# The end of the front stage of a hybrid attention and DeltaNet layer in another order: value tiles, late strips, packed rows and stores

## The chip, the cores and the metric

The kernel runs on one core of a Trainium2 chip. The time is that of one execution on the device, in microseconds (us). A core has a matrix engine (TensorE, PE in the profile, with its weight loads as PEld), a vector engine (VectorE, DVE), a scalar engine (ScalarE, ACT), GpSimd (POOL) and a queue engine that issues transfers (SyncE, SP). The engines run side by side, each works through its own list of instructions in order, and they wait for each other by semaphores.

## What is computed

One layer of a flow-matching backbone, in fp32, over 256 context tokens and 1024 latent tokens (1280 in all, model width 1024). The conditioning vectors give six modulation vectors per token group (`mod = silu(cond) @ w_mod + b_mod`), and one combined projection feeds two mixers:

```
h    = rmsnorm(x, norm_mix) * (1.0 + scale1) + shift1
proj = h @ w_in            # aq, ak, av, dq, dk, dv, dbeta, dalpha, dgate, g_attn, g_dn
aq, ak = rmsnorm per head;  latent tokens also get the axial rotation
o_attn = softmax(rot(aq) @ [cached keys, rot(ak)].T / 8) @ [cached values, av]
o_dn   = gated DeltaNet, both directions, chunks of 64
x = x + gate1 * (sigmoid(g_attn) * (o_attn @ w_attn_br) + sigmoid(g_dn) * (o_dn @ w_dn_br)) @ w_out
x = x + gate2 * moe(rmsnorm(x, norm_ffn) * (1.0 + scale2) + shift2)   # 16 experts, 2 per token
```

The outputs are the final norm of x, and the context tokens' keys, values and DeltaNet states.

## The kernel before

The program is cut into stages. At the end of a stage every engine adds 1 to the semaphore `arrivals` and waits until all five have done so: this is a barrier. Only the **front stage** and its barrier (the first one, `arrivals` 5) are touched. The **attention stage** follows behind it.

The front stage normalises and turns x into `hT` (tokens along the free axis), and makes the first third of the modulation. Then come five tiles of 128 columns of `w_in` (NA = 5: one of keys, `ak`, four of queries, `aq`). A tile goes through these steps:

- `gemm(n)` on PE, line 800; ACT copies the product to SBUF (L1272) and squares it (L1282).
- `ssq(n)` on PE, L826: the sums of squares by head, three column groups of 256, 512 and 512. `roots(n)` on ACT, L1248: their square roots. It waits until tile n-1 is done.
- `norm_tile(n)` on DVE: a reciprocal (L1540), the scaled tile (L1545, signal `y_ready`). `rotate(n)` on PE (L832, two groups of 512) needs that signal. Then DVE multiplies each half with the sine (L1552, signal `rot_used`), multiplies the tile with the cosine (L1554) and adds (L1556, signal `tile_done`).

Beside this run ten **value tiles**, `values_betas(n)` on PE (L847, 16 instructions each: 8 matmuls, in two passes each), which ACT copies out (L1298, L1299). They depend on `hT` and on free PSUM banks alone.

The rest of the modulation comes in eight **late strips**, numbers 4 to 11 of 12. Each is a transfer of 2 MB into one buffer, `wmod_late`, issued by SP (L472) when PE has used the strip before it (`wmod_used`). `late_mod(j)` on PE first turns the result of strip j-1 (`mod_turn`, L732, after ACT has copied it, L1208) and then multiplies strip j (`mod_rows`, L725). `late_mod(12)` turns the last. With that DVE finishes the modulation and packs the rows that later stages need into `row_pack` (L1492, L1496, L1566). PE turns the pack (L879, signal `rows_turned`), DVE copies it (L1576, `mod_ready` 4), and SP stores it in `row_scratch` (L527).

PE also turns the 512 cached keys (L872, needs the last value tile copied) and the context part of the new keys (L876, needs `tile_done` of the last tile). DVE copies both (L1569, and L1572 to `ktok`, which SP stores as an output, L525).

The order of all this is written out by hand. On PE, before: all five tiles with strips 4 to 8 between them; value tiles 0 and 1; `rotate(3)` and `ssq(4)`; value tile 2; then strips 9, 10, 11 behind value tiles 2, 5 and 8; value tile 9; `late_mod(12)`; `rotate(4)`; the turns. SP at the end waits for its stores to land (`sp_out` 64 and `rows_in` 16) before it arrives at the barrier.

Of the kernel before, what the change touches and what calls it, by code (L numbers as in the profile page):

```python
# [19 lines left out]
ACT = mybir.ActivationFunctionType  # L20
AX = mybir.AxisListType

P = 128
# [71 lines left out]
def build(nc, a, outs):  # L95
    ctx = ExitStack()
    with ctx:
# [133 lines left out]
        NA = 5  # L231

        def strips_in(n):
            return 16 * sum(2 if TILES[m][0] == "aq" else 1 for m in range(n % NW, n + 1, NW))
# [45 lines left out]
        ktok = R3[:, 1024:1024 + 2 * P].rearrange("p (n c) -> p n c", c=P)  # L280
# [189 lines left out]
        def _(sp):  # L470
# [50 lines left out]
            for g in range(2):  # L521
                sp.dma_start(outs[3][0, 0, g].rearrange("(n p) d -> p n d", p=P), v_sb[:, 0:2, g * HD:(g + 1) * HD]).then_inc(S["sp_out"], 16)
            sp.wait_ge(S["dve_once"], 3)
            for g in range(2):
                sp.dma_start(outs[2][0, 0, g].rearrange("(n p) d -> p n d", p=P), ktok[:, :, g * HD:(g + 1) * HD]).then_inc(S["sp_out"], 16)  # L525
            sp.wait_ge(S["mod_ready"], 4)
            sp.dma_start(rows_d, pack_turned).then_inc(S["rows_in"], 16)  # L527
            sp.wait_ge(S["sp_out"], 64)
            sp.wait_ge(S["rows_in"], 16)
# [11 lines left out]
            sp.wait_ge(S["sp_out"], 192)  # L541

# [167 lines left out]
        def _(pe):  # L710
# [50 lines left out]
            def late_mod(j):  # L761
                if j - 1 >= EARLY:
                    mod_turn(j - 1, 7, P)
                if j < NMOD:
                    mod_rows(j, 7)
# [94 lines left out]
            for n in range(NT):  # L860
                values_betas(n)
                if n == 1:
                    rotate(NA - 2)
                    ssq(NA - 1)
                if n % 3 == 2:
                    late_mod(EARLY + NA + n // 3)
# [6 lines left out]
            last.then_inc(S["pe_once"], 1)  # L873
            pe.wait_ge(S["tile_done"], NA)
# [3 lines left out]
            pe.wait_ge(S["mod_ready"], 3)  # L878
            mm(ps[0:64, 0, 0:P], row_pack, ident, start=True, stop=True).then_inc(S["rows_turned"], 1)  # L879
# [318 lines left out]
        def _(act):  # L1198
# [3 lines left out]
            def mod_rows(j, bank):  # L1202
                act.wait_ge(S["wmod_used"], j + 1)
                if j - 1 > 0:
                    act.wait_ge(S["mod_turned"], j)
                for q in range(4):
                    r = slice(32 * q, 32 * q + 2)
                    f(mod_row[r, j % 2, :], ps[r, bank, 0:P], ACT.Copy).then_inc(S["mod_row"], 1)  # L1208
# [96 lines left out]
            for n in range(NT):  # L1305
                values_betas(n)
                if n == 3:
                    roots(NA - 1)
                if n % 3 == 2:
                    mod_rows(EARLY + NA + n // 3, 7)  # L1310
# [168 lines left out]
        def _(dve):  # L1479
# [55 lines left out]

            def norm_tile(n):
# [10 lines left out]

                dve.wait_ge(S["past_in"], 96)
# [12 lines left out]
            dve.wait_ge(S["mod_turned"], NMOD + 1)  # L1561
            modulation(4 * EARLY, 4 * NMOD, ps[:, 7, P + 8 * EARLY:P + 8 * NMOD])
            scale_of(A2, 32, norm_ffn)
            for r, src in enumerate((mod[:, 16:24, :], A2[:], mod[:, 24:32, :], mod[:, 40:48, :])):
                signal = "mod_ready" if r == 3 else "dve_chain"
                v.tensor_copy(row_pack[:, 16 * r:16 * r + 16].rearrange("p (c k) -> p k c", c=2), src).then_inc(S[signal], 1)  # L1566
                dve.wait_ge(S[signal], 3 if r == 3 else count(signal))
            dve.wait_ge(S["pe_once"], 1)
            v.tensor_copy(kT[:, T:T + PAST], ps[:, 2, :]).then_inc(S["dve_chain"], 1)  # L1569
            dve.wait_ge(S["dve_chain"], count("dve_chain"))  # L1570
            dve.wait_ge(S["pe_once"], 2)
            v.tensor_copy(flat(ktok), ps[:, 3, 0:2 * P]).then_inc(S["dve_once"], 1)  # L1572
            dve.wait_ge(S["dve_once"], count("dve_once"))

            dve.wait_ge(S["rows_turned"], 1)
            v.tensor_copy(pack_turned, ps[0:64, 0, 0:P]).then_inc(S["mod_ready"], 1)  # L1576
            dve.wait_ge(S["mod_ready"], 4)
# [656 lines left out]
```

## Times and profile before

| | us |
|---|---|
| median of 3 runs | 2327.17 |
| lowest, highest | 2324.61, 2339.4 |
| profiled execution | 2330.84 |
| its span | 2328.9 |
| PE busy in the span | 2119.4 (91%) |
| DVE busy | 992.8 (43%) |
| ACT busy | 627.9 (27%) |
| POOL busy | 251.0 (11%) |

The span is the time from the first to the last instruction of the profiled execution; the rest of its own time lies around it. All times inside are counted from the span's start. PE's granted clock, as a share of full speed, was 0.958 in the mean. Where a row of the trace lists idle time in brackets, that is the engine's idle time just before the row's first instruction, and what ended it.

### The profile page before, as it was taken

How to read it: one execution, taken by the hardware profiler on the slowest of the kernel's cores; microseconds unless marked ns; L12 is line 12 of the kernel's file. 1: busy time of each engine (PE TensorE's matmuls, PEld its weight loads, DVE VectorE, ACT ScalarE, POOL GpSimd, SP SyncE). 2: the span in 40 equal slices, each digit the busy share in tenths (PEclk: the TensorE clock that was granted, in tenths of full speed). 3: DMA queues.
4: the chain of work that ended last, by engine and by line, in shares of the span. 5: the costliest groups of instructions: out<-in, count | busy, mean ns of one | idle time of the engine just before them, and what ended most of it. 6: DMA issues, size and time to landing. Idle time of an engine off the chain costs nothing. (4 is left out here: it accounts for less than half of the span.)

```text
span 2328.9 us, 39352 instructions
## 1 busy us (share of the span) xinstructions
PE 2119.4 (91%) x16471; PEld 1295.2 (56%) x16471; DVE 992.8 (43%) x1846; ACT 627.9 (27%) x1292; POOL 251.0 (11%) x311
## 2 busy tenths in 40 slices
PE   4996899999998889998899999999999689989993
PEld 3555567766554478887654555555455544434441
DVE  3254565652776476667460111001233423323334
ACT  6222666663343233332330000000111011111113
POOL 2000000000000133342000000000000012212220
PEclk8998899999999999999999999999999589999997
DMA  9422200001100223433302211111422656787846
GB/s 332 150 94 90 58 4 2 2 1 55 27 23 5 39 48 65 74 61 51 84 0 73 51 31 27 27 27 46 155 83 98 226 151 171 194 242 207 241 85 207
DMA packets 256381, 210.09 MB, mean 90 GB/s; under 512 B 147468, under 2 KB 219472, under 8 KB 255568
## 3 DMA queue, kind: packets, MB, share of 16 engines
q1 hardware_dynamic: 244912, 168.66, 24.6%
q0 software_dynamic: 11296, 38.92, 7.4%
q8 instruction: 133, 2.18, 0.4%
q14 instruction: 40, 0.33, 0.0%
HBM read 160.14 MB, written 47.25 MB: 89 GB/s over the span
## 5 line engine op out<-in xcount | busy, mean ns | idle before, releaser
L800 PE MATMUL ps<-R 128*128 128x512 f32 (+1 forms) x816 | 297.4, 522 | 5.0 <-DVE R L1526 1.9
L1076 PE MATMUL ps<-R 128*128 128x512 f32 (+1 forms) x768 | 279.5, 522 | 4.4 <-POOLq L2186 2.3
L1160 PE MATMUL ps<-R 128*128 x560 | 255.4, 610 | 16.2 <-SPq L691 13.9
L800 PEld LDWEIGHTS ps<-R 128*128 128x128 f32 x816 | 154.3, 190 | 144.5 <-issue 133.7
L1076 PEld LDWEIGHTS ps<-R 128*128 128x128 f32 x768 | 145.3, 190 | 136.1 <-issue 126.3
L1160 PEld LDWEIGHTS ps<-R 128*128 128x128 f32 x560 | 109.1, 196 | 156.8 <-issue 156.8
L1850 DVE TENSOR_TENSOR R<-ps,R 128x512 f32<-128x512 f32 (+1 forms) x48 | 28.9, 603 | 376.8 <-ACT R L1426 376.0
L1589 DVE TENSOR_SCALAR_CACHE_REDUCE R<-ps 128x512 f32<-128x512 f32 (+1 forms) x208 | 128.4, 666 | 60.1 <-PE ps L896 60.0
L968 PE MATMUL ps<-R 64*64 64x64 f32 x3840 | 130.0, 225 | 24.7 <-DMA R<-tu_scratch 13.0
L968 PEld LDWEIGHTS ps<-R 64*64 64x64 f32 x3840 | 122.8, 140 | 42.5 <-issue 13.7
L1101 PE MATMUL ps<-R 128*128 128x512 f32 x320 | 141.2, 600 | 3.9 <-PEq L1088 3.9
L1081 PE MATMUL ps<-R 128*128 128x512 f32 (+1 forms) x384 | 141.7, 521 | 0.5 <-DMA R<-attn_out_scratch 0.5
L2196 POOL DMA_INDIRECT R<-h_scratch,slot_i x35 | 34.4, 982 | 928.7 <-DVE slot_i L2010 729.3
L1426 ACT ACTIVATE R<-ps 128x512 f32<-128x512 f32 (+1 forms) x48 | 25.2, 526 | 395.1 <-PE ps L1081 394.3
L1170 PE MATMUL ps<-R 128*128 x280 | 126.2, 593 | 1.6 <-DVE R L2053 1.6
L915 PEld LDWEIGHTS ps<-cst,R 128*128 128x128 f32 x800 | 86.4, 142 | 58.9 <-issue 49.7
L2053 DVE COPY R<-ps 128x256 f32<-128x256 f32 x35 | 14.9, 424 | 236.0 <-PE ps L1185 236.0
L915 PE MATMUL ps<-cst,R 128*128 128x128 f32 x800 | 105.1, 279 | 5.7 <-ACT R L1330 2.9
L896 PE MATMUL ps<-R 64*128 64x512 f32 (+1 forms) x416 | 106.5, 616 | 3.5 <-SPq L531 3.3
L1320 ACT ACTIVATE R<-R 128x1536 f32<-128x1536 f32 (+1 forms) x80 | 108.6, 1358 | 3.0 <-DVE R L1598 2.9
L1081 PEld LDWEIGHTS ps<-R 128*128 128x128 f32 x384 | 72.9, 190 | 65.4 <-issue 61.2
L1464 ACT ACTIVATE R<-ps 128x256 f32<-128x256 f32 x35 | 13.4, 384 | 342.7 <-PE ps L1160 342.7
(288 smaller groups left out, 2800.0 us busy)
## 6 DMA issues: line engine op xcount, KB each, us to landing
R<-in_w_mod_dram SPq DMA_DIRECT2D x12, 2048.0 KB, 9.1
R<-in_w_gate_e_dram SPq DMA_DIRECT2D x16, 1024.0 KB, 5.8
R<-in_w_up_e_dram SPq DMA_DIRECT2D x16, 1024.0 KB, 11.2
R<-in_w_down_e_dram SPq DMA_DIRECT2D x16, 1024.0 KB, 13.2
R<-in_w_in_dram SPq DMA_DIRECT2D x30, 512.0 KB, 5.4
R<-tu_scratch SPq DMA_DIRECT2D x80, 128.0 KB, 3.3
R<-in_x_sample_dram SPq DMA_DIRECT2D x16, 512.0 KB, 6.3
lt_scratch<-R SPq DMA_DIRECT2D x40, 128.0 KB, 2.8
```

What stands on the lines that cost most here:

```text
L800: last = mm(ps[:, u % 4, 0:w], w_sb[n % NW][:, k, :], hT[:, k, c0:c0 + w], start=(k == 0), stop=(k == KD - 1))
L896: last = mm(ps[:, 2 * (u % 2) + g, 0:w], qT[lo, h4, qt * P:(qt + 1) * P], kT[lo, c0 + j * 512:c0 + j * 512 + w], start=True, stop=True)
L915: last = turn128(ps[:, 4 + v % 3, k * P:(k + 1) * P], s_sb[i % 2][g][:, j * 512 + k * P:j * 512 + (k + 1) * P], ident)
L968: last = mm(ps[lo, bank, a * C:(a + 1) * C], lhs(a)[lo], rhs(a)[lo], start=start and (alone or a == 0), stop=stop and (alone or a == PAIRS ...
L1076: mm(ps[:, o + x, 0:w], wk[:, x, k, :], hT[:, k, c0:c0 + w], start=(k == 0), stop=(k == KD - 1))
L1081: last = mm(ps[:, o + 2 + x, 0:w], wb[:, x, k, :], (aoT, odT)[x][:, k, c0:c0 + w], start=(k == 0), stop=(k == 3))
L1101: last = mm(ps[:, 2 * (n % 2) + h, :], mT[:, k, n * P:(n + 1) * P], ow[k][:, h * 512:(h + 1) * 512], start=(k == 0), stop=(k == KD - 1))
L1160: last = mm(ps[:, 2 + t % 2, :], hsT[t % 2][:, k, :], R[:, bass.ds(at + (RB + k * 512), 512)], start=(k == 0), stop=(k == KD - 1))
L1170: last = mm(ps[:, 5 + u % 3, :], hidT[t % 2][:, k, :], R[:, bass.ds(at + (RB + 4096 + k * D + h * 512), 512)], start=(k == 0), stop=(k == 1))
L1320: f(s_sb[i % 2][g][:, 0:w], s_sb[i % 2][g][:, 0:w], ACT.Exp, bias=shift[i % 2][g], accum_out=sums[qt % 2][:, g, h4:h4 + 1]).then_inc(S["p_ ...
L1589: v.tensor_scalar(s_sb[i % 2][g][:, j * 512:j * 512 + w], ps[:, 2 * (u % 2) + g, 0:w], HD ** -0.5, None, ALU.mult, ALU.max, accum_out=tops ...
L2196: pool.indirect_dma_start(hs[t % 2], None, h2_d, bass.IndirectOffsetOnAxis(ap=slot_i[:, t:t + 1], axis=0)).then_inc(S[f"hs_in{t % 2}"], 16)
```

## The change

Five things are moved, and one instruction pair is added.

1. PE and ACT: a table `LATE_BEHIND` puts strips 9, 10 and 11 behind value tiles 3, 6 and 9 (before: 2, 5 and 8), and `rotate(3)` with `ssq(4)`, and on ACT `roots(4)`, go behind value tile 4 (before: PE behind value tile 1, ACT behind 3).
2. DVE: finishing the modulation and packing its rows is now a function `rows_modulated()`, called in the last tile's `norm_tile` before its rotation, no longer behind it.
3. PE turns the pack before it turns the context keys; DVE copies the pack before `ktok`; SP stores the pack first.
4. SP no longer waits for its stores before the first barrier. It waits for the rows one barrier later. The buffer of `ktok` moves to a place that the attention stage doesn't write.
5. ACT: an `Exp` of one column, and the wait for it, before the barrier.

```diff
+        LATE_BEHIND = {3: EARLY + NA, 6: EARLY + NA + 1, 9: EARLY + NA + 2}
...
-        ktok = R3[:, 1024:1024 + 2 * P].rearrange("p (n c) -> p n c", c=P)
+        ktok = R3[:, 15040:15040 + 2 * P].rearrange("p (n c) -> p n c", c=P)
@@ sync: the pack's store goes ahead of ktok's
+            sp.wait_ge(S["mod_ready"], 4)
+            sp.dma_start(rows_d, pack_turned).then_inc(S["rows_in"], 16)
             sp.wait_ge(S["dve_once"], 3)
             for g in range(2):
                 sp.dma_start(outs[2][0, 0, g]...ktok...).then_inc(S["sp_out"], 16)
-            sp.wait_ge(S["mod_ready"], 4)
-            sp.dma_start(rows_d, pack_turned).then_inc(S["rows_in"], 16)
-            sp.wait_ge(S["sp_out"], 64)
-            sp.wait_ge(S["rows_in"], 16)
             sp.sem_inc(S["arrivals"], 1)
...
             sp.wait_ge(S["sp_out"], 192)
+            sp.wait_ge(S["rows_in"], 16)
@@ tensor
             for n in range(NT):
                 values_betas(n)
-                if n == 1:
+                if n in LATE_BEHIND:
+                    late_mod(LATE_BEHIND[n])
+                if n == 4:
                     rotate(NA - 2)
                     ssq(NA - 1)
-                if n % 3 == 2:
-                    late_mod(EARLY + NA + n // 3)
             late_mod(NMOD)
             rotate(NA - 1)
...
+            pe.wait_ge(S["mod_ready"], 3)
+            mm(ps[0:64, 0, 0:P], row_pack, ident, start=True, stop=True).then_inc(S["rows_turned"], 1)
             pe.wait_ge(S["tile_done"], NA)
             for n in range(2):
                 last = turn128(ps[:, 3, n * P:(n + 1) * P], kT[:, n * P:(n + 1) * P], ident)
             last.then_inc(S["pe_once"], 1)
-            pe.wait_ge(S["mod_ready"], 3)
-            mm(ps[0:64, 0, 0:P], row_pack, ident, start=True, stop=True).then_inc(S["rows_turned"], 1)
@@ scalar
             for n in range(NT):
                 values_betas(n)
-                if n == 3:
+                if n in LATE_BEHIND:
+                    mod_rows(LATE_BEHIND[n], 7)
+                if n == 4:
                     roots(NA - 1)
-                if n % 3 == 2:
-                    mod_rows(EARLY + NA + n // 3, 7)
+            f(stat[:, 63:64], one_c, ACT.Exp).then_inc(S["act_chain"], 1)
+            act.wait_ge(S["act_chain"], count("act_chain"))
@@ vector: the body of rows_modulated() stood behind the loop over norm_tile
+                if n == NA - 1:
+                    rows_modulated()
                 dve.wait_ge(S["past_in"], 96)
                 for g in (1, 2):
                     dve.wait_ge(S["rot_mm"], 2 * n + g)
```

On PE, from the first value tile to the turn of the last strip. `R` is the large SBUF buffer, `ps` PSUM; L847 is a value tile (x16 is two tiles of 8 matmuls), L732 a turn, L725 a strip, L832 a rotation, L826 the sums of squares. Before:

```order
L847 MATMUL ps<-R 128x160 x16
L832 MATMUL ps<-R,cst 128x512 x2
L826 MATMUL ps<-R,cst 128x256
L826 MATMUL ps<-R,cst 128x512 x2
L847 MATMUL ps<-R 128x160 x8
L732 MATMUL ps<-cst,mod_row 128x8
L725 MATMUL ps<-R,cond_s 2x128 x32
L847 MATMUL ps<-R 128x160 x24
L732 MATMUL ps<-cst,mod_row 128x8
L725 MATMUL ps<-R,cond_s 2x128 x32
L847 MATMUL ps<-R 128x160 x24
```

And after the change, where every line number of this part is one higher:

```order
L848 MATMUL ps<-R 128x160 x32
L733 MATMUL ps<-cst,mod_row 128x8
L726 MATMUL ps<-R,cond_s 2x128 x32
L848 MATMUL ps<-R 128x160 x8
L833 MATMUL ps<-R,cst 128x512 x2
L827 MATMUL ps<-R,cst 128x256
L827 MATMUL ps<-R,cst 128x512 x2
L848 MATMUL ps<-R 128x160 x16
L733 MATMUL ps<-cst,mod_row 128x8
L726 MATMUL ps<-R,cond_s 2x128 x32
L848 MATMUL ps<-R 128x160 x24
```

Value tiles 2, 3 and 4 and strip 9 now stand ahead of the rotation of tile 3. Behind the last rows shown come, before, the last strip, a value tile, the last turn and the last rotation; after, the last strip, the last turn and the last rotation, with no value tile between.

On DVE, the last tile from its reciprocal on, and the packing (L1492 to L1566 before). Before:

```order
L1540 RECIPROCAL R<-R 128x1280 [waits root_ready,tile_done]
L1545 SCALAR_TENSOR_TENSOR R<-R,prm 128x256 [waits dve_chain]
L1545 SCALAR_TENSOR_TENSOR R<-R,prm 128x1024 [waits dve_chain]
L1552 TENSOR_TENSOR R<-ps,R 128x512 [waits rot_mm,past_in,y_ready]
L1552 TENSOR_TENSOR R<-ps,R 128x512 [waits rot_mm,rot_used]
L1554 TENSOR_TENSOR R<-R 128x1024 [waits rot_used]
L1556 TENSOR_TENSOR R<-R 128x1024 [waits dve_chain]
L1492 TENSOR_TENSOR mod<-ps,prm 128x64 [waits mod_turned,tile_done]
```

After:

```order
L1552 RECIPROCAL R<-R 128x1280 [waits root_ready,tile_done]
L1557 SCALAR_TENSOR_TENSOR R<-R,prm 128x256 [waits dve_chain]
L1557 SCALAR_TENSOR_TENSOR R<-R,prm 128x1024 [waits dve_chain]
L1495 TENSOR_TENSOR mod<-ps,prm 128x64 [waits mod_turned,y_ready]
L1499 SCALAR_TENSOR_TENSOR A<-mod,prm 128x16 [waits dve_chain]
L1545 COPY R<-mod 128x8x2 [waits dve_chain]
L1545 COPY R<-A 128x8x2 [waits dve_chain]
L1545 COPY R<-mod 128x8x2 [waits dve_chain] x2
L1566 TENSOR_TENSOR R<-ps,R 128x512 [waits rot_mm,past_in,mod_ready]
```

The six small instructions of the packing, and their wait for the last strip's turn (`mod_turned`), now stand between the scaled tile and its rotation's products.

On SP, from the stores of the context values to the first load of the attention stage. Before:

```order
L522 DMA out_dram<-R 128x2x64
L525 DMA out_dram<-R 128x2x64 [waits dve_once]
L525 DMA out_dram<-R 128x2x64
L527 DMA row_scratch<-R 64x128 [waits mod_ready]
L501 DMA R<-in_w_in_dram 128x8x128 [waits sp_out,rows_in,arrivals]
```

After:

```order
L524 DMA out_dram<-R 128x2x64
L526 DMA row_scratch<-R 64x128 [waits mod_ready]
L529 DMA out_dram<-R 128x2x64 [waits dve_once]
L529 DMA out_dram<-R 128x2x64
L503 DMA R<-in_w_in_dram 128x8x128 [waits arrivals]
```

The store of the pack is first, and the first load behind the barrier no longer waits for stores.

## Rows read from the trace of the kernel before

**Rows 1.** Busy time by stretch: start:end, length, engines' busy us, granted clock, DMA share, GB/s.

```profile
172.59:237.97 65.38, 43.67 (x389) 35.01 (x389) 32.37 (x25) 14.45 (x48) 0.00 (x0) 0.83 0.28 96
237.97:560.00 322.03, 314.39 (x2886) 216.06 (x2887) 186.78 (x591) 198.97 (x351) 21.49 (x27) 0.99 0.07 20
```

**Rows 2.** Timeline of PE: start us, us, operation, count, idle before it and its end.

```profile
174.81 4.51 PE L847 MATMUL ps<-R 128*128 128x160 f32 x32
188.45 3.74 PE L832 MATMUL ps<-R,cst 128*128 128x512 f32 x4 [9.13 <-DVE R L1545]
193.13 2.39 PE L826 MATMUL ps<-R,cst 128*128 128x256 f32 x6 [0.94 <-DVE R L1552]
...
197.53 0.28 PE L732 MATMUL ps<-cst,mod_row 128*128 128x8 f32 x2
197.74 1.93 PE L725 MATMUL ps<-R,cond_s 128*2 128x128 f32 x64
...
208.78 3.37 PE L725 MATMUL ps<-R,cond_s 128*2 128x128 f32 x64 [2.27 <-DMA R<-in_w_mod_dram]
...
221.41 2.39 PE L725 MATMUL ps<-R,cond_s 128*2 128x128 f32 x64 [2.24 <-DMA R<-in_w_mod_dram]
...
227.31 1.96 PE L832 MATMUL ps<-R,cst 128*128 128x512 f32 x4
...
237.97 2.08 PE L896 MATMUL ps<-R 64*128 64x256 f32 x8 [3.30 <-SPq L531]
```

**Rows 3.** Timeline of DVE in the same stretch.

```profile
192.29 0.69 DVE L1552 TENSOR_TENSOR R<-ps,R 128x512 f32<-128x512 f32 x1 [0.94 <-PE ps L832]
...
194.28 1.22 DVE L1556 TENSOR_TENSOR R<-R 128x1024 f32<-128x1024 f32 x1
204.35 8.15 DVE L1540 RECIPROCAL R<-R 128x1280 f32<-128x1280 f32 x1 [8.84 <-ACT R L1248]
212.54 1.81 DVE L1545 SCALAR_TENSOR_TENSOR R<-R,prm 128x256 f32<-128x256 f32 x2
228.55 1.52 DVE L1552 TENSOR_TENSOR R<-ps,R 128x512 f32<-128x512 f32 x2 [14.21 <-PE ps L832]
...
232.62 0.22 DVE L1492 TENSOR_TENSOR mod<-ps,prm 128x64 f32<-128x64 f32 x1
...
233.96 0.69 DVE L1569 COPY R<-ps 128x512 f32<-128x512 f32 x1
234.68 0.42 DVE L1572 COPY R<-ps 128x256 f32<-128x256 f32 x1
235.14 0.28 DVE L1576 COPY R<-ps 64x128 f32<-64x128 f32 x1
```

**Rows 4.** Timeline of ACT in the same stretch.

```profile
202.33 1.92 ACT L1248 ACTIVATE R<-ps,epsc 128x256 f32<-128x256 f32 x3
...
223.84 1.14 ACT L1208 ACTIVATE mod_row<-ps 2x128 f32<-2x128 f32 x4 [4.39 <-PE ps L725]
```

**Rows 5.** Timeline of SP's queue in the same stretch.

```profile
199.73 12.82 SPq L472 DMA_DIRECT2D R<-in_w_mod_dram  x2
...
235.13 0.89 SPq L525 DMA_DIRECT2D out_dram<-R  x2
236.06 0.54 SPq L527 DMA_DIRECT2D row_scratch<-R  x1
```

**Rows 6.** DMA issues of 150 to 262 us: KB each, median us from issue to landing.

```profile
row_scratch<-R SPq DMA_DIRECT2D x1, 32.0 KB, 1.8
```

**Rows 7.** Timeline of ACT, first rows behind the barrier.

```profile
240.26 1.28 ACT L1320 ACT_TABLE_LOAD   x1 [12.53 <-DVE R L1598]
241.56 0.51 ACT L1320 ACTIVATE R<-R 128x256 f32<-128x256 f32 x1
```

**Rows 8.** Timeline of PE behind the barrier.

```profile
242.21 1.18 PE L915 MATMUL ps<-cst,R 128*128 128x128 f32 x4 [2.17 <-ACT R L1320]
243.32 1.22 PE L896 MATMUL ps<-R 64*128 64x256 f32 x4
...
246.57 0.71 PE L896 MATMUL ps<-R 64*128 64x256 f32 x4
...
248.46 0.70 PE L896 MATMUL ps<-R 64*128 64x256 f32 x4
```

**Rows 9.** Busy time by stretch, columns as in group 1: clock before and behind the barrier.

```profile
234.00:236.00 2.00, 0.67 (x2) 0.27 (x2) 1.35 (x3) 0.00 (x0) 0.00 (x0) 0.50 0.00 0
...
248.00:250.00 2.00, 1.98 (x18) 1.07 (x20) 0.76 (x8) 1.89 (x8) 0.11 (x1) 1.00 1.19 291
```

More of the change, by code:

```diff
@@ L1534, in _, with rows_modulated @@
             SEG = [(0, 256, 1), (256, 1024, 259)]
+            def rows_modulated():
+                dve.wait_ge(S["mod_turned"], NMOD + 1)
+                modulation(4 * EARLY, 4 * NMOD, ps[:, 7, P + 8 * EARLY:P + 8 * NMOD])
+                scale_of(A2, 32, norm_ffn)
+                for r, src in enumerate((mod[:, 16:24, :], A2[:], mod[:, 24:32, :], mod[:, 40:48, :])):
+                    signal = "mod_ready" if r == 3 else "dve_chain"
+                    v.tensor_copy(row_pack[:, 16 * r:16 * r + 16].rearrange("p (c k) -> p k c", c=2), src).then_inc(S[signal], 1)
+                    dve.wait_ge(S[signal], 3 if r == 3 else count(signal))
             def norm_tile(n):
@@ L1560, in _ @@
                 norm_tile(n)
[L1561 to L1567, printed above, removed]
             dve.wait_ge(S["pe_once"], 1)
@@ L1570, in _ @@
             dve.wait_ge(S["dve_chain"], count("dve_chain"))
+            dve.wait_ge(S["rows_turned"], 1)
+            v.tensor_copy(pack_turned, ps[0:64, 0, 0:P]).then_inc(S["mod_ready"], 1)
+            dve.wait_ge(S["mod_ready"], 4)
             dve.wait_ge(S["pe_once"], 2)
@@ L1573, in _ @@
             dve.wait_ge(S["dve_once"], count("dve_once"))
-            dve.wait_ge(S["rows_turned"], 1)
-            v.tensor_copy(pack_turned, ps[0:64, 0, 0:P]).then_inc(S["mod_ready"], 1)
-            dve.wait_ge(S["mod_ready"], 4)
             dve.sem_inc(S["arrivals"], 1)
```

## The prediction

> **What bounds the kernel now.** I read the page first: PE is busy 91% of the span. The table of stretches shows where it is not: in the last 65.38 us of the front stage, from the sums of squares of tile 3 to the first scores of attention, PE is busy 43.67 us, and 21.7 us are idle; in the 322.03 us behind it, it is busy 314.39 [rows 1]. So what this stage loses is lost to the kernel, and what is saved here is kept as long as the next stages are bound by PE and by nothing that runs on a clock of its own. I then read the timelines of PE, DVE, ACT and SP side by side.
>
> PE's idle pieces are: 9.13 us for the scaled tile 3, 0.94 for its rotation's products, 2.27 and 2.24 for strips, and at the end the wait for DVE and the stores, of which 3.30 us stand in front of the first scores and name SP [rows 2]. Two chains lead to the barrier. The **tile chain**: tile 3 done at 195.50 (194.28 + 1.22), roots of tile 4 only at 202.33, reciprocal at 204.35, scaled tile at 214.35 (212.54 + 1.81), and then DVE idles 14.21 us because PE comes to `rotate(4)` only at 227.31 [rows 2 to 4]. The **strip chain**: strip 10 is issued at 199.73 and used from 208.78, 9.05 us later; strip 11 is issued at about 212.2 (the end of that row's 12.82 us, less an issue) and used from 221.41, 9.2 us later [rows 2, 5]. PE's own order holds both: `rotate(4)` stands behind all value tiles and strips, and strip 9 is used at 197.74 though PE idled before 188.45. The attention stage then begins with a table load on ACT, 1.28 us, and PE waits 2.17 us for that exponential [rows 7, 8].
>
> **The change step by step.** Times are worked out on this trace's axis.
>
> *The 9.13 us gap is filled.* A value tile takes 4.51 / 2 = 2.26 us, turn and strip together 2.1 us (from 197.53 to 199.67) [rows 2]. From 174.81: four value tiles to 183.85, strip 9 to 185.95, value tile 4 to 188.2. The scaled tile 3 comes when it did, and PE rotates at 188.45. So 8.9 us of work move into idle time and delay nothing, with 0.25 us to spare. If the cover were too short, the excess would be paid once in the tile chain only.
>
> *Rotation of tile 3 at full clock.* Behind the gap it took 3.74 us; `rotate(4)` out of a busy stretch took 1.96 [rows 2]. By the second, the first product is there 1.24 us after the start (227.31 to 228.55), and DVE needs 4.07 us from there until it is free again (228.55 to 232.62) [rows 2, 3]. Tile 3 is done at 188.45 + 1.24 + 4.05 = 193.7, 1.8 us sooner.
>
> *Tile 4.* `ssq(4)` follows at 191.35 and ends at 193.75 (2.39 us); the roots need tile 3 done, and now stand behind value tile 4's copy, long past. They take 1.92 us to 195.7 [rows 2, 4]. Reciprocal and scaling take 10.0 us (204.35 to 214.35) [rows 3]: scaled tile at 205.8, 8.5 us sooner.
>
> *The strips.* Strip 10 is issued when strip 9 is used, 185.95, and lands by 195. PE goes on at 193.75: value tiles 5 and 6 to 198.2, strip 10 to 200.3. Strip 11 is issued there and lands 9.05 to 9.2 us later, 209.4. Value tiles 7 to 9 take PE to 207.1, so it waits 2.2 us, as it does now. The strip took 3.37 and 2.39 us behind such waits [rows 2]; I take 2.9: 212.3. ACT's copy takes 1.14 [rows 4] and nothing covers it any more, since value tile 9 has gone ahead: 213.5. The turn is there at 213.7, against 227.4 now. That is the pacemaker of the new order: the strip chain, not the tile chain, which has been ready for 8 us.
>
> *Packing ahead of the last rotation.* It costs DVE 1.34 us (232.62 to 233.96) [rows 3] whichever way; now it lies beside `rotate(4)`, whose first product needs 1.24 us. DVE begins on the products at 215.05 and is free at 219.1, if the array runs at full clock. At half clock the second product comes 3.84 us after the start (188.45 to 192.29) [rows 2, 3], and this step is 1.6 us longer. PE is busy from 209.4 but for 1.2 us, so I take the first.
>
> *The tail.* DVE still has the copies of the cached keys, the pack and `ktok`: 0.69, 0.28 and 0.42 us [rows 3], with gaps 1.5 us, to 220.6. What PE turns in between is covered by them: the pack during the tile's last two products, the keys during the first copy. SP issues the pack's store (0.54) at 220.1 and `ktok`'s two (0.89) from 220.7 [rows 5], and arrives at 221.6. It waits for no landing, where now the barrier opens only when the store issued at 236.06 has landed, 1.8 us later [rows 5, 6]. First scores at 221.8 instead of 237.97: **16.2 us**. Queued behind these stores are only loads that the DeltaNet stage uses, and the new wait for the rows stands behind a wait for eight transfers that SP issues in the middle of attention: both nothing. The moved `ktok` costs nothing.
>
> *The table load.* ACT has nothing to do from 215 to 221.8, so a load and an `Exp` of one column are covered there. PE's wait of 2.17 us behind the barrier shrinks by the load, **1.3 us** [rows 7, 8]; were the cover gone it would be worth nothing, not less. Behind it ACT uses exponential and copies as before.
>
> The Trainium skill ("ScalarE: Activation LUTs", section "What ACT_TABLE_LOAD costs") gives 1283 ns for the load and about 1380 ns for a drain, 2.66 us for a switch. The trace agrees on the load and shows no drain on this path: the load starts at 240.26, and the exponential at 241.56. By the page the sum would be 1.4 us larger; I take the row.
>
> *The clock at the start of attention.* It is at half (1.2 GHz) from before the barrier on and back at full (2.4 GHz) by 248 [rows 9]. At half, one round from scores to scores took 3.25 us (243.32 to 246.57), at full 1.9 (246.57 to 248.46) [rows 8]. PE goes into the barrier as idle as now, so I take no change; a round sooner or two is 1.3 to 2.6 us of gain, a round later 1.3 of loss.
>
> Sum: 16.2 + 1.3 = 17.5 us. Against the profiled execution's own time, 2330.84, that is 2313.3. That execution lies 3.7 us above the median of 2327.17, and the change is compared with such medians: 2327.17 - 17.5 = 2309.7, said as **2310**. Its own range: the upper side has the half clock (1.6), the strip at 3.37 us (0.5), a later clock (1.3) and the median's own place (lowest run 2324.61, highest 2339.4); the lower side the earlier clock (2.6) and the lowest run (2.6). That gives 2305 to 2315.
>
> **The rivals.**
>
> *The late strips pace it worse than worked out.* Everything behind strip 11 now hangs on a 9 us transfer with no work beside it but three value tiles, and DVE holds the finished tile 4 back until its turn. For it: both strips are waited for already [rows 2]. Against it: the load has its queue alone, and took 9.05 and 9.2 us. With a strip of 11 us twice, the half clock and the longer strip, the gain falls to 17.5 - 2 - 1.6 - 0.5 - 1, about 12.5: 2315. Chance 0.13.
>
> *Nothing is kept.* The barrier opens earlier, but the attention or a later stage runs into a date that doesn't move. For it there is no row: all five engines start the attention stage from the barrier, SP loads for it nothing, and PE is at 314.39 of 322.03 [rows 1]. The same result would come if another engine reached the barrier late. 2326. Chance 0.05.
>
> *More is kept.* The filled gap and the shorter wait keep the array's clock high into the attention stage, two rounds of 1.3 us at its start, and a drain that the trace hides goes as well: 17.5 + 4 = 21.5, 2305.5. Chance 0.10.
>
> *Slower.* The place is the start of the attention stage: the clock does not come back there. A round costs 1.3 us more at half clock [rows 8], so it takes 14 such rounds in a row to eat the 17.5 us, and more from there on to be slower; with 20 rounds the time is 2310 + 26 = 2336. For it: one of three runs of the same kernel took 2339.4, so some executions lose 12 us somewhere. Against it: the mean granted clock of the stretch behind the barrier is 0.99, the cold start included [rows 1], and its work isn't changed. Chance 0.03.
>
> **How the numbers follow.** The forecast has 0.69, the rivals 0.13, 0.05, 0.10 and 0.03. The likeliest time is 2310. The range starts at 2304, just below the case where more is kept, and ends at 2317, above the case of slow strips; it leaves out the case where nothing is kept, the slower one, and the tails. A measurement of this kernel can tell about 1%, 23 us, from no change. The whole sum is 0.75% of the time, so within 1% has nearly everything: faster by over 1% would need 2303.9 or less, a tail of the case where more is kept, 0.04; slower by over 1% needs 2350, 0.02; within 1%, 0.94.
>
> **What would show it.** In the changed profile PE should have no idle of more than 1 us between 174.8 and 188.4, and the rotation of tile 3 should take about 2 us instead of 3.74. The reciprocal of tile 4 should start near 195.8, strip 11 should be used from near 209.4 with 2 us of wait before it, the last rotation start near 213.6, and the first scores near 221.8, released by SP or DVE; the table load should stand before the barrier, and PE's wait behind the first scores be 0.9 us. The prediction is wrong if value tiles 2 to 4 overrun 188.45 by more than 1 us, if a strip's load takes well over 9.2 us now that it starts at another time, if the first scores move by 16 us and the last instruction does not, or if the clock behind the barrier differs by more than two rounds.

## The result and the profile after

The median after the change is 2315.36 us (6 runs, 2311.09 to 2316.06), beside 2330.94 us before (6 runs, 2324.61 to 2339.4). The medians are 15.6 us apart. The ratio found by comparing the runs is 0.9925, with a 95% interval of 0.9908 to 0.9942: a gain of 17.5 us, 13.5 to 21.4. The profiled execution took 2312.47 us, 18.4 us less than that of before. The forecast was 2310 us, with a sum of 17.5 us.

First the busy time by stretch: from the sums of squares of tile 3 to the first scores, and the same length behind them as in [rows 1]. The columns are start:end, length, busy us of PE, PEld, DVE, ACT and POOL, granted clock, DMA share, GB/s.

```profile
172.37:220.27 47.90, 38.34 (x389) 32.12 (x389) 32.36 (x25) 15.95 (x50) 0.00 (x0) 0.98 0.37 128
220.27:542.30 322.03, 315.59 (x2888) 216.64 (x2889) 186.76 (x591) 197.68 (x350) 21.49 (x27) 0.99 0.07 20
```

The stretch is 17.48 us shorter (65.38 to 47.90) with the same 389 matmul instructions. PE's idle time in it fell from 21.7 to 9.6 us, 12.1 us less. The other 5.3 us are busy time, 43.67 to 38.34: the same work at a granted clock of 0.98 instead of 0.83. The stretch behind it has the same granted clock in both, 0.99; PE is busy 1.2 us more in the same length. I call the start of the sums of squares of tile 3 **the mark** (172.59 before, 172.37 here), since executions differ by up to 3 us ahead of it (171.93 to 174.85 in all profiles of this text).

PE's timeline after the change, from the mark:

```profile
172.37 2.39 PE L827 MATMUL ps<-R,cst 128*128 128x256 f32 x6 [0.94 <-DVE R L1566]
174.59 8.86 PE L848 MATMUL ps<-R 128*128 128x160 f32 x64
...
183.50 1.93 PE L726 MATMUL ps<-R,cond_s 128*2 128x128 f32 x64
185.35 2.44 PE L848 MATMUL ps<-R 128*128 128x160 f32 x16
188.22 1.98 PE L833 MATMUL ps<-R,cst 128*128 128x512 f32 x4 [0.43 <-DVE R L1557]
...
208.46 1.93 PE L726 MATMUL ps<-R,cond_s 128*2 128x128 f32 x64 [1.76 <-DMA R<-in_w_mod_dram]
211.65 0.39 PE L733 MATMUL ps<-cst,mod_row 128*128 128x8 f32 x2 [1.26 <-ACT mod_row L1209]
211.90 1.96 PE L833 MATMUL ps<-R,cst 128*128 128x512 f32 x4
...
217.47 0.44 PE L879 MATMUL ps<-cst,R 128*128 128x128 f32 x2 [2.81 <-DVE R L1570]
220.27 2.08 PE L897 MATMUL ps<-R 64*128 64x256 f32 x8 [2.35 <-SPq L531]
223.23 1.18 PE L916 MATMUL ps<-cst,R 128*128 128x128 f32 x4 [0.89 <-ACT R L1323]
224.34 1.22 PE L897 MATMUL ps<-R 64*128 64x256 f32 x4
```

Against [rows 2]: the gap of 9.13 us is 0.43; the rotation behind it takes 1.98 us, no longer 3.74; only one strip is waited for, 1.76 us, and the wait for ACT's copy that follows, 1.26 us, is new. Behind the first scores PE waits 0.89 us for ACT, where it waited 2.17 [rows 8]; the next scores (L897) still take 1.22 us, the half clock.

DVE, around the last tile and the packing:

```profile
195.57 8.15 DVE L1552 RECIPROCAL R<-R 128x1280 f32<-128x1280 f32 x1 [2.05 <-ACT R L1249]
...
212.15 0.23 DVE L1495 TENSOR_TENSOR mod<-ps,prm 128x64 f32<-128x64 f32 x1 [6.58 <-PE ps L733]
...
213.48 1.42 DVE L1566 TENSOR_TENSOR R<-ps,R 128x512 f32<-128x512 f32 x2
...
218.49 0.42 DVE L1582 COPY R<-ps 128x256 f32<-128x256 f32 x1
```

The reciprocal starts 8.8 us sooner than in [rows 3]. DVE then has the scaled tile at 205.57 and waits 6.58 us for the last strip's turn.

SP and ACT at the end of the stage:

```profile
218.49 0.54 SPq L526 DMA_DIRECT2D row_scratch<-R  x1
219.07 1.09 SPq L529 DMA_DIRECT2D out_dram<-R  x2
220.28 7.49 SPq L503 DMA_DIRECT2D R<-in_w_in_dram  x6
```

```profile
210.46 1.14 ACT L1209 ACTIVATE mod_row<-ps 2x128 f32<-2x128 f32 x4 [3.47 <-PE ps L726]
211.62 1.28 ACT L1312 ACT_TABLE_LOAD   x1
212.91 0.20 ACT L1312 ACTIVATE stat<-epsc 128x1 f32<-128x1 f32 x1
```

SP's last issue ends at 220.16, and the first load behind the barrier starts at 220.28: nothing waits for a landing. The table load has moved from the first softmax [rows 7] into ACT's idle time.

### The profile page after: what moved, and what is told of

Its sections match the earlier page's. It is cut to its first block and busy times, and to the rows that moved or that the text cites. A ratio compares the mean times of both kernels' runs of the same rounds, so it can differ in the third digit from the quotient of the medians.

```text
span 2310.5 us, 39353 instructions
## 1 busy us (share of the span) xinstructions
PE 2116.4 (92%) x16471; PEld 1296.2 (56%) x16471; DVE 993.0 (43%) x1846; ACT 628.1 (27%) x1293; POOL 250.1 (11%) x311
## 3 DMA queue, kind: packets, MB, share of 16 engines
q8 instruction: 133, 2.18, 0.4%
## 5 line engine op out<-in xcount | busy, mean ns | idle before, releaser
L897 PE MATMUL ps<-R 64*128 64x512 f32 (+1 forms) x416 | 106.9, 618 | 2.5 <-SPq L531 2.4
```

The lines of the kernel that those rows point to most:

```text
L897: last = mm(ps[:, 2 * (u % 2) + g, 0:w], qT[lo, h4, qt * P:(qt + 1) * P], kT[lo, c0 + j * 512:c0 + j * 512 + w], start=True, stop=True)
```

## The experiments

Places are given from each run's own mark, so that the different starts drop out. The table has the three places that matter; all come from PE's timelines.

| kernel | last rotation | first scores | from rotation to scores | PE's wait for ACT behind them |
|---|---|---|---|---|
| before | 54.72 | 65.38 | 10.66 | 2.17 |
| before, second profile | 55.53 | 66.19 | 10.66 | 2.17 |
| changed | 39.53 | 47.90 | 8.37 | 0.89 |
| changed, second and third profile | 39.75, 39.22 | 48.12, 47.59 | 8.37, 8.37 | 0.89, 0.89 |
| order on PE and ACT alone | 39.66 | 50.32 | 10.66 | 2.16 |
| stores alone | 52.56 | 62.03 | 9.47 | 2.17 |
| changed, no table load ahead | 39.42 | 47.80 | 8.38 | 2.17 |
| changed, packing behind | 39.86 | 49.41 | 9.55 | 0.89 |
| changed, strip 10 early | 36.38 | 44.75 | 8.37 | 0.89 |
| the same, last rotation early, packing behind | 33.96 | 43.44 | 9.48 | 0.89 |
| before, last rotation moved alone | 46.15 | 58.76 | 12.61 | 2.17 |

### The order alone

```diff
 the kernel before, with
+        LATE_BEHIND = {3: EARLY + NA, 6: EARLY + NA + 1, 9: EARLY + NA + 2}
 and the changed loops over values_betas on PE and on ACT; nothing else
```

> The kernel before with the new order on PE and ACT alone (strips 9, 10, 11 behind value tiles 3, 6, 9; rotation and sums behind value tile 4); packing, stores and table load as before. Measured from the start of the sums of squares of tile 3, the first scores came 65.4 us later before and 47.9 us later after the change. Theory (the order on PE is nearly the whole gain): the last rotation starts as in the changed kernel, 39.5 us behind that mark; from the first product on DVE to the first scores it takes 9.4 us as before, so the first scores come at 39.5 + 1.2 + 9.4 = 50.2 us, a gain of 15.3 of the 17.5. Rival (the stores' landings and the packing are a large part): first scores at 54 or later. PE's wait for ACT behind the first scores stays 2.2 us.

PE's timeline of this run:

```profile
213.12 1.96 PE L834 MATMUL ps<-R,cst 128*128 128x512 f32 x4
...
223.78 2.08 PE L898 MATMUL ps<-R 64*128 64x256 f32 x8 [3.30 <-SPq L533]
```

The first scores stand 50.32 us behind the mark, 0.1 from the theory. From the rotation to them it takes the same 10.66 us as before, and the 3.30 us of [rows 2] are there to the hundredth. The order on PE and ACT is worth 15.06 of the 17.48 us. Which part of that is PE's order and which is ACT's (`roots(4)` on ACT started only at 202.33 [rows 4], although tile 3 was done at 195.50 [rows 3]) no run separates. The execution took 2317.47 us.

### The stores alone

```diff
 the kernel before, with
+        ktok = R3[:, 15040:15040 + 2 * P]...
 the pack turned, copied and stored ahead of ktok, and
-            sp.wait_ge(S["sp_out"], 64)
-            sp.wait_ge(S["rows_in"], 16)
```

> The kernel before with the stores' part alone: the pack turned, copied and stored first, no wait for landings before the barrier, ktok's buffer moved; order on PE and ACT, packing behind the last tile and table load as before. Theory: the barrier's opening moves by the landing less what the stores' issue still costs: DVE done at 235.4, the last store issued by 236.5, first scores at 236.6 instead of 237.97, so 64.0 us behind the mark instead of 65.4, a gain of 1.4. Rival (the stall is worth the whole 3.3 us that PE spends for SP): first scores 62.1 us behind the mark.

```profile
208.24 0.28 PE L731 MATMUL ps<-cst,mod_row 128*128 128x8 f32 x2
210.55 3.37 PE L724 MATMUL ps<-R,cond_s 128*2 128x128 f32 x64 [2.02 <-DMA R<-in_w_mod_dram]
...
227.41 1.96 PE L831 MATMUL ps<-R,cst 128*128 128x512 f32 x4
...
236.88 2.08 PE L895 MATMUL ps<-R 64*128 64x256 f32 x8 [1.97 <-SPq L529]
```

Read from the mark, 62.03 is the rival's number, 62.1. It is the wrong ruler here, and the expectation should not have used it: the edit touches nothing ahead of the last rotation, yet that stands at 52.56 instead of 54.72 in this execution (shorter waits for strips, 2.02 and 2.20 us, and, at full clock this time, the last strip with 1.93 us instead of 2.39 and above all the value tile behind it with 2.44 instead of 3.61). Behind the rotation, where the edit lies, 10.66 us became 9.47: the stores' part is worth 1.19 us. PE's wait marked with SP fell from 3.30 to 1.97 and did not vanish, since PE waits there for DVE's copies and SP's issues too. The Trainium skill ("DMA: Bandwidth & Descriptors", section "Rules for kernel authors") says to wait on a transfer's semaphore late, so that its fixed cost overlaps. The runs agree on the direction; of the 1.8 us from issue to landing [rows 6] 1.19 came back. The rest is mostly the issue itself, 0.54 us, which still has to be done: SP's last issue ends 1.25 us behind DVE's last copy here (235.53 to 236.78), 1.18 before (235.42 to 236.60).

### The changed kernel without the table load ahead

```diff
 the changed kernel, without
-            f(stat[:, 63:64], one_c, ACT.Exp).then_inc(S["act_chain"], 1)
-            act.wait_ge(S["act_chain"], count("act_chain"))
```

> The changed kernel without the Exp of one column. Theory: first scores stay 47.9 us behind the mark, the table load of 1.28 us is again behind them, and PE's wait for ACT there is 2.2 us instead of 0.9; everything behind is 1.3 us later. Rival (a drain of another 1.4 us is paid at such a switch, or the load is covered by DVE's reductions): the wait grows by 2.7 us, or not at all.

ACT's timeline, and then PE's:

```profile
222.67 1.28 ACT L1321 ACT_TABLE_LOAD   x1 [10.97 <-DVE R L1602]
223.97 0.51 ACT L1321 ACTIVATE R<-R 128x256 f32<-128x256 f32 x1
```

```profile
220.38 2.08 PE L897 MATMUL ps<-R 64*128 64x256 f32 x8 [2.36 <-SPq L531]
224.62 1.18 PE L916 MATMUL ps<-cst,R 128*128 128x128 f32 x4 [2.17 <-ACT R L1321]
```

The load is worth 1.28 us in PE's wait, 2.17 against 0.89. The expectation's "everything behind is 1.3 us later" was too much: from the first scores to the last of the stage it takes 295.4 us here and 294.6 in the changed kernel, 0.8 more. The rival with a drain, which the Trainium skill ("ScalarE: Activation LUTs", section "What ACT_TABLE_LOAD costs") puts at about 1380 ns on top, is refuted for this place: the exponential starts 0.02 us behind the load, and the load starts as soon as DVE's row maximum for the softmax is there. This execution took 2309.89 us, less than the changed kernel's 2312.47, although it lost 1.28 us here. A single execution can't show such a term; its place in the trace can.

### The packing behind the last tile again

```diff
 the changed kernel, with rows_modulated() called behind the loop over norm_tile:
-                if n == NA - 1:
-                    rows_modulated()
```

> The changed kernel with the packing behind the last tile's rotation again (order of PE and ACT, stores and Exp as changed). Theory: the packing's 1.34 us lie beside the rotation's first product in the changed kernel and on the path here; the products start 0.3 us sooner, so the first scores come 1.0 us later, 48.9 us behind the mark. Rival (DVE is not on the path to the barrier, SP is): no change, 47.9.

```profile
212.73 1.96 PE L833 MATMUL ps<-R,cst 128*128 128x512 f32 x4
...
222.28 2.08 PE L897 MATMUL ps<-R 64*128 64x256 f32 x8 [1.57 <-SPq L531]
```

From the rotation to the first scores it takes 9.55 us instead of 8.37: the packing ahead of the rotation's products is worth 1.18 us. DVE is on the path to the barrier. The place from the mark, 49.41, is 0.5 later than expected; 0.33 of that is the last rotation's own place in this execution.

### Strip 10 early

```diff
 the changed kernel, with
-        LATE_BEHIND = {3: EARLY + NA, 6: EARLY + NA + 1, 9: EARLY + NA + 2}
+        LATE_BEHIND = {3: EARLY + NA, 8: EARLY + NA + 2}
                 if n == 4:
                     rotate(NA - 2)
                     ssq(NA - 1)
+                    late_mod(EARLY + NA + 1)
 and the same on ACT
```

> The changed kernel with another order on PE and ACT: strip 10 right behind the sums of squares of tile 4 (in the changed kernel behind value tile 6), strip 11 behind value tile 8 (there behind 9). Theory (the chain of late strips paces the new order): strip 11 is issued 4.4 us sooner and lands before PE has done value tiles 5 to 8, so PE's wait of 1.8 us for it is gone, and value tile 9 covers ACT's copy of its result, so most of the 1.3 us wait for ACT is gone too: last rotation 2.7 us sooner, first scores about 45.2 us behind the start of the sums of squares of tile 3 instead of 47.9. Rival (the chain of tile 4 through ACT and DVE paces): the last rotation stays where it is, 39.5 us behind the mark, or moves by less than 0.5 us. In time 2.7 us is 0.12%, at the edge of what five rounds can tell.

```profile
193.98 1.93 PE L726 MATMUL ps<-R,cond_s 128*2 128x128 f32 x64
195.84 8.96 PE L848 MATMUL ps<-R 128*128 128x160 f32 x64
204.64 0.28 PE L733 MATMUL ps<-cst,mod_row 128*128 128x8 f32 x2
204.85 1.93 PE L726 MATMUL ps<-R,cond_s 128*2 128x128 f32 x64
206.71 2.44 PE L848 MATMUL ps<-R 128*128 128x160 f32 x16
208.99 0.28 PE L733 MATMUL ps<-cst,mod_row 128*128 128x8 f32 x2
209.13 1.96 PE L833 MATMUL ps<-R,cst 128*128 128x512 f32 x4
```

No row in this stretch has idle time ahead of it: both waits, 1.76 and 1.26 us, are gone, and the last rotation and the first scores stand 3.15 us sooner. In the changed kernel the chain of late strips was the pacemaker, not tile 4. The median is 2310.31 us (2306.87 to 2315.63, 5 runs), the ratio to before 0.9910 (0.9897 to 0.9924).

### The last rotation early as well

```diff
 the kernel above, with
                 if n in LATE_BEHIND:
                     late_mod(LATE_BEHIND[n])
+                if n == NT - 2:
+                    rotate(NA - 1)
...
             late_mod(NMOD)
-            rotate(NA - 1)
 and the packing behind the last tile again
```

> The kernel of the early strip with the last rotation behind strip 11 and ahead of value tile 9 and the last turn, and the packing behind the tile's rotation. Theory (the scaled tile 4 lies ready for 3 us and more before PE comes to it): rotation 2.3 us sooner again, the packing's 1.3 us back on DVE's path behind it: first scores 1.0 us sooner than with the early strip alone, 44.2 us behind the mark, 3.7 us sooner than in the changed kernel. Rival (the last strip's turn decides whatever stands where): no gain over the early strip alone, or a loss of up to 1.3 us.

```profile
208.48 1.98 PE L833 MATMUL ps<-R,cst 128*128 128x512 f32 x4
210.30 2.34 PE L848 MATMUL ps<-R 128*128 128x160 f32 x16
...
217.96 2.08 PE L899 MATMUL ps<-R 64*128 64x256 f32 x8 [1.99 <-SPq L531]
```

The mark of this run is 174.52. The first scores stand at 43.44, another 1.31 us sooner. In DVE's timeline the scaled tile 4 is ready 33.22 us behind the mark, and the rotation starts at 33.96: the last rotation now follows tile 4 by 0.74 us, so the next thing in the way is the tile chain itself.

That lead is not kept through the attention stage. The same instructions there, behind the same wait, in the kernel with the early strip alone and then in this one:

```profile
280.94 1.50 PE L917 MATMUL ps<-cst,R 128*128 128x128 f32 x12 [1.83 <-ACT R L1335]
281.92 2.62 PE L918 MATMUL ps<-cst,R 128*128 128x128 f32 x12 [1.83 <-ACT R L1336]
```

The granted clock is 1.00 behind the first wait (281 to 285) and 0.53 and then 0.62 behind the second (282 to 284, 284 to 286). The second profile of this kernel has the same dip (2.79 us for these instructions, clock 0.55 and 0.60); the other eleven profiles take 1.50 us there. The last scores of the stage start 340.3 us behind the mark here, 339.5 with the early strip alone and 342.5 in the changed kernel. So at the end of the scores the early rotation is 0.8 us behind the early strip alone, and its lead over the changed kernel is 2.2 us. Why the clock falls there only with this order was not tried.

The median is 2306.58 us (2301.92 to 2309.3, 4 runs), the ratio 0.9881 (0.9866 to 0.9897).

### The last rotation moved alone

```diff
 the kernel before, with
+                if n == 8:
+                    rotate(NA - 1)
...
             late_mod(NMOD)
-            rotate(NA - 1)
```

> The kernel before with one call moved: the last rotation on PE stands behind value tile 8 instead of behind the last strip's turn. Nothing is filled into the gap ahead of tile 3's rotation, strips and stores as before. Theory (the two chains meet at PE's own order): DVE finishes tile 4 while PE waits for strip 11, so the last turn, 54.6 us behind the start of the sums of squares of tile 3, is followed at once by the packing, and from the packing's start to the first scores it takes 5.35 us as before: first scores 60.0 us behind the mark instead of 65.4. The remaining 12 us to the changed kernel are then the strips' own lateness, which only the filled gap takes away. Rival (order around the last tile is worth most of the gain): first scores 55 us behind the mark or sooner; or nothing at all, 65.4.

```profile
218.86 1.88 PE L832 MATMUL ps<-R,cst 128*128 128x512 f32 x4
...
221.59 1.93 PE L725 MATMUL ps<-R,cond_s 128*2 128x128 f32 x64 [0.73 <-DMA R<-in_w_mod_dram]
...
231.47 2.08 PE L897 MATMUL ps<-R 64*128 64x256 f32 x8 [3.55 <-SPq L531]
```

The mark is 172.71, the first scores stand at 58.76, 6.6 us sooner than before and 1.2 sooner than the theory. On DVE the packing starts at 226.12, the first scores come 5.35 us later, exactly as before; what differs from the theory is the last turn, at 53.02 instead of 54.58, since the last strip and the value tile behind it ran at full clock this time (1.93 and 2.44 us instead of 2.39 and 3.61). Of the 17.5 us, between 5.4 and 6.6 were there for moving one call. The rest, 11 to 12, needed the strips to come sooner, and so the gap to be filled.

### The changed kernel again, and the kernel before again

> The changed kernel, unchanged, once more beside the kernel before. The forecast's sum of 17.5 us is a ratio of 0.9925. If what the front stage saves is kept and nothing else differs, the ratio of this comparison is 0.9920 to 0.9930 and its profile has the first scores 47.9 us behind the mark; if part of it is given back later, the ratio is above 0.994.

The median is 2315.27 us (5 runs), before 2332.68 (15 runs in the same rounds), 17.4 us apart; the ratio 0.9917 (0.9904 to 0.9931), 19.4 us.

> The kernel before, unchanged, for a second profile of it: its runs so far lie between 2324.6 and 2339.4 us. If they differ by transfers that the last stages wait for, the front stage is the same to 0.5 us (first scores 65.4 us behind the mark) and the difference stands in the waits of the expert stage behind 1600 us; if the clock makes it, the mean granted clock differs in some stretch.

The second profile of the kernel before has a span of 2338.3 us, 9.4 more than the first. Its mark is 172.36 and its first scores stand at 66.19, 0.8 us later than in the first: the sums of squares of tile 4 took 4.61 us instead of 2.39, at half clock, and the last strip and value tile, at full clock, gave part of it back. PE's waits in the DeltaNet stage (780 to 1160 us), of the first profile and then of the second, with us in total, times and longest:

```profile
PE ps L1026 <- DVE R L1815: 17.8, 9, 5.5
PE ps L968 <- DMA R<-tu_scratch: 13.0, 8, 6.1
PE ps L968 <- DVE R L1776: 7.0, 7, 1.9
```

```profile
PE ps L1026 <- DVE R L1815: 20.7, 9, 5.6
PE ps L968 <- DMA R<-tu_scratch: 6.7, 7, 2.3
PE ps L968 <- DVE R L1776: 6.6, 7, 1.9
PE ps L968 <- SPq L582: 5.9, 1, 5.9
```

From the stage's first matmul of L968 to the first of L1045 it took 334.0 us in the first and 340.2 in the second. In the changed kernel's three profiles it took 335.1, 334.9 and 339.6. The wait of some 6 us that turns up here for SP is also in executions with a short stage, there for a transfer. So I can name the place, the DeltaNet stage, and that a same kernel differs there by 6 us, but not the cause. The expert stage is the other such place: from the first matmul of L1160 to the last of L1185, 420.1 and 420.3 us before, 417.8 and 421.0 and 419.8 after, and 415.4 in the kernel with the packing behind, none of which changes anything there. The expectation had looked for a wait behind 1600 us only, and for a front stage that is the same to 0.5 us, and was wrong in both.

In the same rounds the kernel before was compared with itself: ratio 0.9985, interval 0.9974 to 0.9996. That interval leaves out 1, which it should not. So the intervals of this kernel are too narrow, by 0.04% or 1 us at the least.

> The version with the early strip and the early last rotation again, in the same rounds as the changed kernel. Its first scores were 4.5 us sooner than in the changed kernel, its median 8.7 us lower. If only the front stage counts, this comparison gives medians 4 to 6 us apart; if the order makes a later stage shorter too, 8 us or more, with a shorter DeltaNet or expert stage in the profile.

> The changed kernel again, for the comparison with the version with early strip and early rotation. Ratio to the kernel before 0.9917 to 0.9925, as in the two comparisons so far.

The changed kernel: median 2317.18 us (2307.54 to 2322.05, 6 runs), ratio 0.9926 (0.9904 to 0.9949). The version with early strip and early rotation: 2309.53 us (2306.19 to 2315.32, 6 runs), ratio 0.9903 (0.9884 to 0.9923). The first scores are 4.14 us apart from the mark (43.45 and 47.59), the medians 7.7. Here the intervals overlap. In the two comparisons the version's median is 8.7 and 7.7 us lower. The front stage gives 4.7 and 4.1 of it, and by the last scores of the attention stage 2.6 and 2.3 are left. Its DeltaNet stage is hardly shorter or not at all (336.3 and 338.9 us, beside 334.9 and 339.6), its expert stage took 415.4 and 415.0 us, beside 421.0 and 419.8. So in these profiles most of the difference stands in the expert stage. It is as short (415.4 and 415.5) in the kernels with the stores alone, without the table load ahead and with the packing behind, none of which changes anything there, so the excess may be scatter; it stays open.

## Why the prediction was right

**The place and the sum.** The sum was 17.5 us. In the profiles the first scores moved by 17.48 from the mark, where 16.2 had been worked out, and the wait behind them by 1.28, 18.8 together. By the last scores of the attention stage it is 18.5 (361.0 and 342.5 us behind the mark), and the spans differ by 18.4. By comparison of runs it is 17.5, 19.4 and 17.3 us (ratios 0.9925, 0.9917, 0.9926), and by the medians 15.6, 17.4 and 15.1. So it is kept to the end, and the case where nothing is kept is refuted. The mechanism is right, and by the places the sum is 1.3 us too small. That the first comparison gives the forecast's 17.5 to the tenth is luck: its interval is 13.5 to 21.4, and the place of the last rotation alone lies between 52.56 and 55.53 us in the three profiles with the order of before.

**Filling the gap.** Right, with 0.43 us to spare instead of 0.25: the value tiles 2 to 4 and strip 9 took PE to 187.79.

**Rotation of tile 3 at full clock.** Right: 1.98 us for 3.74, in every kernel that fills the gap, and 3.47 to 3.78 in every kernel that doesn't.

**The pacemaker.** Right that the strip chain paces the new order and tile 4 does not, shown by the kernel with strip 10 early (3.15 us). Two terms of it were sized too large. The load of strip 11, from issue to use, took 8.5 us (issued at 199.93 by SP's timeline, used from 208.46), where 9.05 to 9.2 had been read. And the strip took 1.93 us, where I had put 2.9, between the 2.39 and 3.37 of before: the array stayed at full clock through the wait. The granted clock was 1.00 from 206 to 218. With both, ACT's copy was done 1.7 us sooner behind the mark than worked out. The turn behind it took 0.39 us where 0.2 had been counted, and DVE began the packing 39.78 us behind the mark instead of 41.1, 1.3 us sooner. Since the packing's wait for that turn holds DVE, the products followed 1.35 us sooner (41.11 instead of 42.46). The scaled tile 4 came as worked out (205.57, forecast 205.8) and lay ready for 6.3 us.

**The packing.** Its 1.34 us were put beside the rotation's first product. Measured, moving it is worth 1.18 us (packing behind: 9.55 against 8.37 from rotation to scores).

**The tail.** From the first product to the first scores 6.79 us, worked out 6.75. Of the stores I had given no price of their own ahead of the result; the expectation said 1.4, and the run alone gave 1.19.

**The table load.** 1.28 us, put at 1.3. By the figure for a whole switch that the Trainium skill gives ("ScalarE: Activation LUTs", section "What ACT_TABLE_LOAD costs") this term would have been put 1.4 us too large.

**The clock at the start of attention.** Taken as unchanged, which was right to 0.3 us. From the first row of scores to the third it took 8.60 us before (237.97 to 246.57) and 7.32 after (220.27 to 227.59), 1.28 less, the table load. One round later the difference is 1.03 (10.49 and 9.46), and at the last scores of the stage 1.0 (295.6 and 294.6): the third scores after the change still ran mostly at the half clock, 1.04 us where [rows 8] has 0.71. The other profiles say the same: from the first scores to the last it takes 294.1 to 294.9 us in the five with the table load ahead and no early rotation, and 295.3 to 296.4 in the six without it, in the mean 1.05 apart. So of the table load's 1.28 us some 1.0 is kept; the slower case and the case where more is kept both fell away.

**The level.** The forecast of 2310 stood on the median of three runs, 2327.17. With more runs of before the medians were 2330.9 to 2332.7, 4 to 5 us higher, and the changed kernel's 2315.3 to 2317.2. The measured 2315.4 lies inside the range of 2304 to 2317, but just above the 2305 to 2315 that the forecast's own case was given. The range took it in because it was widened for the rival of slow strips, which had the same time, 2315. Its mechanism did not come: the load of strip 11 took less than worked out, not more. So the time alone could not tell the two apart, the trace does. The size of the step was forecast better than its foot.

The pieces, each from its own run: order on PE and ACT 15.06 (with its effect on the clock), stores 1.19, packing 1.18, table load 1.28, together 18.7, against 18.8 in the profiles of the whole. The last three lie one behind the other on one path, so they should add up, and the stores, measured on the kernel before, are worth about the same on the new order (10.66 to 9.55 us from rotation to scores, 1.11). That the sum fits to 0.1 us rests on the pair of profiles: against the second profile of before the order is worth 15.9, and with the last rotation's place of the kernel with the stores alone 12.9.

## What to carry to other kernels

When two chains end at one barrier and the engine between them works through a list in fixed order, write down for each chain when its next input is ready and when the engine comes to it; the difference is what an order can give, and the chain whose input comes last is the next pacemaker. Work that depends on nothing belongs into the gap ahead of a wait; work that starts a long transfer belongs as early as its buffer allows, or the transfer is waited for at the end. For terms of 1 to 3 us in a kernel whose executions differ by 15, measure places in the trace, from a mark just ahead of the edit to a place just behind it, in more than one profile, and once more at the end of the next stage: there the clock had given back 0.3 us of one term, and 2 us of the early rotation's lead.

## What the runs showed that was not expected

- **The same strip on PE at two speeds behind nearly the same wait.** Strips 10 and 11 took 3.36 to 3.50 us behind waits of 2.27, 2.37, 2.02 and 2.44 us, and 1.93 behind waits of 2.18, 2.20, 2.08 and 1.98. In the first the array was at the lower of its two levels (1.2 GHz; granted clock 0.50 from 210 to 212 in the first profile of before), in the second at 2.4 GHz (1.00 from 206 to 218 in the changed kernel). One lies between: strip 11 in the first profile of before, 2.39 us behind 2.24. All four slow ones are strip 10, the first to be waited for, in the kernels that don't fill the gap; all four fast ones are strip 11. The length of the wait doesn't tell them apart; what does was not tried. In the profiles of the kernels that fill the gap the strip behind the wait always ran at the higher level.
- **A load of 2 MB takes 7.6 to 9.2 us** from issue to landing, in the same stage and with its queue alone. The load of strip 9 took 7.6 to 8.4 in all thirteen profiles. The loads of strips 10 and 11 took 8.8 to 9.2 in the four of kernels that don't fill the gap, and in the nine of those that do 7.7 to 8.1 (strip 10) and 8.1 to 8.8 (strip 11). What makes them shorter there was not tried.
- **Executions of one kernel differ by 6 us in the DeltaNet stage**, with the same instructions. Of the 9.4 us between the two profiles of before 6.2 stand there. The expert stage, unchanged in all, took between 415.0 and 421.0 us in the thirteen profiles. The fastest and the slowest run of before are 16 us apart; what makes all of it the two profiles don't show.
